# Seven-product layers of a two-block transformer: down products dealt between units, the sixth product added in the second bank, later raw loads and low parts

## The reference, cut to what matters

```
# first block (D_FF = 4096)
x = x + jnp.square(jax.nn.relu(h2 @ w_ff1)) @ w_ff2
# second block, twice (D_FF_2 = 2816)
x = x + (silu(h @ w_gate) * (h @ w_up)) @ w_down
```

## Time and profile before

| | |
|---|---|
| median of 3 runs | 2162.22 us (2161.79 to 2162.78) |
| the profiled execution's own time | 2162.55 us |
| its span, first to last instruction | 2160.8 us |
| TensorE matmuls busy | 2106.1 us, 97% |
| weight loads busy | 1730.6 us, 80% |
| VectorE, ScalarE, GpSimd busy | 1506.4, 1040.7, 416.9 us |
| stage 0, 1, 2 begin near | 569, 1171 and 1790 us of the span |

### The profile page before, as it was taken

The page is one execution under the profiler, slowest core; times in us unless marked ns, Lnnn a source line. Parts: engine busy times, 40 slices in busy tenths (PEclk is TensorE's granted clock), DMA queues, the critical chain, the costliest instruction groups (busy, mean ns, idle before and its releaser), DMA issues.

```text
span 2160.8 us, 31657 instructions
## 1 busy us (share of the span) xinstructions
PE 2106.1 (97%) x12528; PEld 1730.6 (80%) x12528; DVE 1506.4 (70%) x2197; ACT 1040.7 (48%) x1754; POOL 416.9 (19%) x350
## 2 busy tenths in 40 slices
PE   9999999999989999999999999999999999999999
PEld 7768777778769899877777788989877667789988
DVE  5674775655577777665576888887556777888885
ACT  4464445554444343434455445545445564545453
POOL 0000422211112323010010134343011101143340
PEclk9999999999999999999999999999999999999999
DMA  4212112123322232222112323222221113222222
GB/s 171 86 49 88 60 53 93 49 85 114 105 98 96 100 118 89 65 92 69 60 58 77 109 88 118 79 98 79 91 85 60 58 49 107 98 98 90 106 107 69
DMA packets 45938, 187.18 MB, mean 87 GB/s; under 512 B 5216, under 2 KB 5728, under 8 KB 40032
## 3 DMA queue, kind: packets, MB, share of 16 engines
q1 hardware_dynamic: 45648, 184.98, 24.8%
q10 hardware_dynamic: 144, 0.18, 0.0%
HBM read 183.05 MB, written 2.10 MB: 86 GB/s over the span
## 4 chain that ended last, share of the span: by engine, by line
PE 85%; DVE 8%; ACT 3%; issue 2%; DMA 1%; SPq 0%; POOL 0%; DVEq 0%; ACTq 0%
PE ps L1252 14%; PE ps L1255 14%; PE ps L1258 14%; PE ps L1326 7%; PE ps L1332 6%; PE ps L1329 6%; PE ps L1276 4%; PE ps L1279 4%; PE ps L1277 4%; PE ps L1231 3%; PE ps L1384 1%; DMA raw<-in_weights 1%; DVE wl L2129 1%; PE ps L1436 1%; PE ps L1657 1%
## 5 line engine op out<-in xcount | busy, mean ns | idle before, releaser
L1716 ACT CAST wh<-raw 128x1024 fp32r<-128x1024 f32 (+1 forms) x246 | 257.6, 1047 | 419.9 <-PE ps L1258 312.2
L2756 POOL TENSOR_TENSOR Q<-Q 128x512 f32<-128x512 f32 x176 | 280.1, 1592 | 807.4 <-DMA Q<-in_sevens 797.1
L2129 DVE TENSOR_TENSOR wl<-raw,wh 128x1024 fp32r<-128x1024 f32 (+2 forms) x250 | 316.9, 1268 | 161.9 <-ACT wh L1716 161.5
L1252 PE MATMUL ps<-R,wh 128*128 128x512 f32 x892 | 288.2, 404 | 7.3 <-ACT wh L1716 5.4
L1255 PE MATMUL ps<-R,wl 128*128 128x512 f32 x892 | 278.2, 392 | 2.8 <-DVE wl L2129 2.6
L1258 PE MATMUL ps<-R,wh 128*128 128x512 f32 x892 | 276.4, 390 | 0.0
L1252 PE MATMUL ps<-hh,wh 128*128 128x512 f32 x704 | 231.3, 409 | 2.7 <-issue 0.8
L1255 PE MATMUL ps<-hh,wl 128*128 128x512 f32 x704 | 219.4, 393 | 12.5 <-DVE wl L2129 12.5
L1258 PE MATMUL ps<-hl,wh 128*128 128x512 f32 x704 | 217.6, 390 | 0.0
L1255 PEld LDWEIGHTS ps<-R,wl 128*128 128x128 f32 x892 | 167.5, 188 | 41.4 <-DVE wl L2129 5.4
L1252 PEld LDWEIGHTS ps<-R,wh 128*128 128x128 f32 x892 | 159.5, 189 | 48.8 <-issue 10.8
(11 more groups left out here) (281 smaller groups left out, 3697.7 us busy)
## 6 DMA issues: line engine op xcount, KB each, us to landing
raw<-in_weights SPq DMA_DIRECT2D x244, 512.0 KB, 3.5
Q<-in_sevens SPq DMA_DIRECT2D x44, 1024.0 KB, 4.9
x<-in_x_t SPq DMA_DIRECT2D x4, 512.0 KB, 7.0
F<-in_x_t SPq DMA_DIRECT2D x4, 512.0 KB, 4.8
out<-x SPq DMA_DIRECT2D x7, 256.0 KB, 2.0
raw<-in_weights SPq DMA_DIRECT2D x4, 416.0 KB, 3.1
x<-in_bias SPq DMA_DIRECT2D x1, 1024.0 KB, 6.9
F<-in_weights SPq DMA_DIRECT2D x2, 384.0 KB, 3.6
```

What stands on the lines that cost most here:

```text
L1252: pe.matmul(out, hi[:, k, cs], B.tile(u.src, k)[0], start=k == 0, stop=False)
L1716: act.copy(B.wh[s][:, 0:nk * ncol], B.raw[s][:, 0:nk * ncol]).then_inc(S["w_hi"], 1)
L2129: dve.tensor_tensor(lo, src, hi.bitcast(F32), ALU.subtract).then_inc(S[name], 1)
L2756: pool.tensor_tensor(B.weight_part(u.v, out), B.weight_part(u.v, a), B.weight_part(u.v, b), op).then_inc(S["w_s"], 1)
```

## The change: what it does

1. `chain`: the down units of the chunk before are dealt out evenly behind the `Seven` units of the next: stages 1 and 2 run G d U d G d U d. Stage 0 has two up units per chunk and keeps its order.
2. Product 5 is accumulated in q's second half, onto product 3 (no start flag), after the copy out of q. Product 4 is copied out of p by ScalarE (a third `wcp`, 128x256), and product 6 waits for that copy. Three `wc` additions are left of four. Bank 3 is free, and down tiles rotate over four banks instead of three.
3. `tile_low` of ordinary tiles is a step of its own, one piece later, behind that piece's `split_low`.
4. `preparation`: new piece numbers; `wq` and `ws` of the second unit five pieces later in stage 0 and two in stages 1 and 2.

```
@@ gated
+        if u.ev in ("relu2", "fup"):
+            self.defer(1, "tile_low", u)
@@ Plan.seven
-        if k in (2, 5):
-            first.append(("wc", u, {2: 1, 5: 2}[k]))
+        if k == 2:
+            first.append(("wc", u, 1))
         if k == 5:
-            self.defer(1, "wc", u, 3)
+            first.append(("wcp", u, 3))
+            self.defer(1, "wc", u, 2)
...
         if k == 6:
-            self.defer(1, "wc", u, 4)
+            self.defer(1, "wc", u, 3)
@@ preparation
+        plain = stage == 0
+        end = 32 if plain else 48
         for m in range(8):
-            put((13, 14, 15, 17, 18, 19, 21, 22)[m], "hn", v, stage, m)
+            put(((13, 14, 16, 17, 18, 20, 21, 22) if plain else (14, 15, 17, 18, 20, 21, 23, 24))[m], "hn", v, stage, m)
         put(14, "ws", wins[0])
         for k in range(4):
-            put((21, 24, 26, 28)[k], "t_sum", stage, k)
-            put((25, 26, 28, 30)[k], "t_hi", stage, k)
-        end = 32 if stage == 0 else 48
-        for k in range(4):
-            put((29, 33, 34, 35)[k] if stage == 0 else (30, 33, 37, 41)[k], "t_lo", stage, k)
+            put(((22, 24, 25, 27) if plain else (26, 28, 30, 32))[k], "t_sum", stage, k)
+            put(((24, 25, 27, 28) if plain else (28, 29, 31, 33))[k], "t_hi", stage, k)
+            put(((28, 29, 30, 33) if plain else (34, 36, 38, 40))[k], "t_lo", stage, k)
...
             put(end + i, "b_hi", stage, i, last_up)
-            put(end + 1 + i + (3 if stage == 0 else 0), "b_lo", stage, i)
-        put(end + 4, "wq", wins[1])
-        put(end + 4, "ws", wins[1])
+            put(end + 2 + i, "b_lo", stage, i)
+        put(end + (9 if plain else 6), "wq", wins[1])
+        put(end + (9 if plain else 6), "ws", wins[1])
@@ chain
-                n = len(ff[c][0]) // 2
-                out += ff[c][0][:n] + ff[c - 1][1][:2] + ff[c][0][n:] + ff[c - 1][1][2:]
+                n = len(ff[c - 1][1]) // len(ff[c][0])
+                for i, u in enumerate(ff[c][0]):
+                    out += [u] + ff[c - 1][1][n * i:n * i + n]
@@ banks of the down units
-                        u.banks.append(turn % 3)
+                        u.banks.append(turn % 4)
@@ tensor_program.seven
         elif k == 5:
-            empty(3)
+            at.wait_ge("w_cp", 3 * u.v + 2)
         elif k == 6:
-            at.wait_ge("w_c", 4 * u.v + 2)
+            at.wait_ge("w_cp", 3 * u.v + 3)
         out = {0: B.bank[q][:, first], 2: B.bank[q][:, first], 3: B.bank[q][:, second],
-               5: B.bank[3][:, second if half else first]}.get(k, B.bank[p][:, first])
+               5: B.bank[q][:, second]}.get(k, B.bank[p][:, first])
...
-            pe.matmul(out, hi[:, n, :], high[:, n, :], start=n == 0 and k not in (4, 6), stop=False, skip_group_check=True)
+            pe.matmul(out, hi[:, n, :], high[:, n, :], start=n == 0 and k not in (4, 5, 6), stop=False, skip_group_check=True)
@@ seven_copy
-        else:
+        elif n == 2:
             at.wait_ge("w_mm", u.product(3) + 1)
             act.copy(b[:], q).then_inc(S["w_cp"], 1)
+        else:
+            at.wait_ge("w_mm", u.product(4) + 1)
+            act.copy(a[:, 256:512], p[:, 0:256]).then_inc(S["w_cp"], 1)
@@ combine
         elif n == 2:
-            at.wait_ge("w_cp", 2 * v + 2)
-            at.wait_ge("w_mm", u.product(4) + 1)
-            dve.tensor_tensor(a[:, 256:512], p[:, 0:256], b[:, 256:512], ALU.add).then_inc(S["w_c"], 1)
-        elif n == 3:
+            at.wait_ge("w_cp", 3 * v + 3)
             at.wait_ge("w_mm", u.product(5) + 1)
-            at.wait_ge("w_c", 4 * v + 2)
-            dve.tensor_tensor(a[:, 256:512], r, a[:, 256:512], ALU.add).then_inc(S["w_c"], 1)
+            dve.tensor_tensor(a[:, 256:512], q[:, 256:512], a[:, 256:512], ALU.add).then_inc(S["w_c"], 1)
```

More of the change, by code:

```diff
@@ L1303, in seven @@
     def seven(u, k):
-        i, (p, q), half = u.product(k), u.banks(), u.v % 2
+        i, (p, q) = u.product(k), u.banks()
         if k == 0:
@@ L1310, in seven @@
         elif k == 2:
-            at.wait_ge("w_cp", 2 * u.v + 1)
+            at.wait_ge("w_cp", 3 * u.v + 1)
         elif k == 4:
-            at.wait_ge("w_c", 4 * u.v + 1)
+            at.wait_ge("w_c", 3 * u.v + 1)
         elif k == 5:
-            empty(3)
+            at.wait_ge("w_cp", 3 * u.v + 2)
         elif k == 6:
-            at.wait_ge("w_c", 4 * u.v + 2)
+            at.wait_ge("w_cp", 3 * u.v + 3)
         first, second = slice(0, 256), slice(256, 512)
         out = {0: B.bank[q][:, first], 2: B.bank[q][:, first], 3: B.bank[q][:, second],
-               5: B.bank[3][:, second if half else first]}.get(k, B.bank[p][:, first])
+               5: B.bank[q][:, second]}.get(k, B.bank[p][:, first])
         (hi, lo), (high, low), name = B.operand(u.place(i)), B.tokens(PRODUCTS[k][1]), PRODUCTS[k][1]
@@ L1333, in seven @@
         last.then_inc(S["w_mm"], 1)
[L1334 to L1337, removed]
+        if k == 6:
+            emptied[p], emptied[q] = (("w_c", 3 * u.v + 3),), (("w_c", 3 * u.v + 2),)
     def mm(u, i, a, b):
@@ L1859, in seven_sigmoid @@
             at.wait_ge("f_lo", u.others[1].arg["tile"])
-        at.wait_ge("w_c", 4 * u.v + 3 + t)
+        at.wait_ge("w_c", 3 * u.v + 2 + t)
         act.activation(to[:], B.W[u.tiles()[t]][:], ACT.Exp, scale=-1.0).then_inc(S["w_sig"], 1)
@@ L1867, in seven_copy @@
     def seven_copy(u, n):
-        q = B.bank[u.banks()[1]]
+        p, q = (B.bank[b] for b in u.banks())
         a, b = (B.W[i] for i in u.tiles(2 if u.ev == "up" else 0))
@@ L2300, in ev @@
                                          op1=ALU.mult).then_inc(S["ev_d"], 1)
-                tile_low(u, B.W[4 + n % 4])
             elif u.ev == "fgate":
@@ L2309, in ev @@
                 dve.tensor_tensor(w[:], bank[:], w[:], ALU.mult).then_inc(S["ev_d"], 1)
-                tile_low(u, w)
             elif u.ev == "up":
@@ L2323, in ev_low, with tile_low @@
         normed_low(u.arg["norm"], u.arg["m"] + j)
-    def tile_low(u, w):
+    def tile_low(u):
+        w = B.W[4 + u.arg["tile"] % 4 if u.ev == "relu2" else u.arg["wk"]]
         hi, lo = B.pair(("f", u.arg["f"]))
@@ L2365, in combine @@
     def combine(u, n):
-        p = B.bank[u.banks()[0]]
-        r, v = B.bank[3][:, 256:512] if u.v % 2 else B.bank[3][:, 0:256], u.v
+        (p, q), v = (B.bank[b] for b in u.banks()), u.v
         a, b = (B.W[i] for i in u.tiles(2 if u.ev == "up" else 0))
         if n == 1:
-            at.wait_ge("w_cp", 2 * v + 1)
+            at.wait_ge("w_cp", 3 * v + 1)
             at.wait_ge("w_mm", u.product(1) + 1)
@@ L2373, in combine @@
         elif n == 2:
-            at.wait_ge("w_cp", 2 * v + 2)
-            at.wait_ge("w_mm", u.product(4) + 1)
-            dve.tensor_tensor(a[:, 256:512], p[:, 0:256], b[:, 256:512], ALU.add).then_inc(S["w_c"], 1)
-        elif n == 3:
+            at.wait_ge("w_cp", 3 * v + 3)
             at.wait_ge("w_mm", u.product(5) + 1)
-            at.wait_ge("w_c", 4 * v + 2)
-            dve.tensor_tensor(a[:, 256:512], r, a[:, 256:512], ALU.add).then_inc(S["w_c"], 1)
+            dve.tensor_tensor(a[:, 256:512], q[:, 256:512], a[:, 256:512], ALU.add).then_inc(S["w_c"], 1)
         else:
+            at.wait_ge("w_cp", 3 * v + 2)
             at.wait_ge("w_mm", u.product(6) + 1)
@@ L2699, in vector_program @@
             "h_score": h_score, "h_fin": h_fin, "h_low": h_low, "c_norm": c_norm, "c_turn": c_turn, "c_qt": c_qt, "c_kv": c_kv,
-            "c_kt": c_kt, "sb": sb, "dn_sum": dn_sum, "dn_mul": dn_mul, "wo_lo": weight_low, "hn": normed, "t_sum": token_sums, "t_lo": token_low,
+            "c_kt": c_kt, "sb": sb, "dn_sum": dn_sum, "dn_mul": dn_mul, "wo_lo": weight_low, "hn": normed, "t_sum": token_sums, "tile_low": tile_low, "t_lo": token_low,
             "b_lo": part_low, "wc": combine, "wf": seven_value, "wf_lo": seven_low}
```

## The result

The changed kernel takes 2146.28 us, median of 4 runs (2145.89 to 2148.74), beside 2162.36 us for the kernel before on the same chip: a ratio of 0.9927, 95% interval 0.9912 to 0.9942. It is faster by 16.1 us, where I had forecast 29 with a range of 17 to 44. The profiled execution took 2146.68 us with a span of 2145.0, so 15.9 us less than that of before.

What follows compares the result with a forecast made beforehand. TensorE's matmuls, busy 97% of the span, were taken as the bound. Gains of 9.8 + 14.5 + 1.8 + 2.8 = 28.9 us from the profiled 2162.55, less 0.33, gave 2133 us; forecast range 2126 to 2138, chance 0.50.

Steps and rivals of the forecast that it cites:

- stage 0's opening: Stage 0, pieces 9 to 48: later `wq` and earlier chunk low parts win 14.5 us in all.
- stages 1 and 2, pieces 16 to 48: Openings of stages 1 and 2: late low parts of chunks go, winning 5.1 and 6.1 us.
- product 6's waits: Product 6 of U in stages 1 and 2 stops waiting for VectorE, 14 times; all 19.6 us go.
- piece 48 to product 2: From piece 48 to product 2 of the first G, stages 1 and 2: 0.6 us lost in each.
- low clock behind the new waits: After 4.5 us waits at the first G in stages 1 and 2, the clock drops: 2.7 us lost each.
- Dealing the down units: Product 2 of a G behind a down unit waits for a ScalarE copy: 0.7 us at 14 places, 9.8 us lost.
- the prediction's own formula: Lateness of product 2 of G: `split`'s start after VectorE's last addition, plus 1.89, minus 6.76 us.
- Sums in the tail everywhere: Rival: GpSimd's sums stretch U's tail at all 14 places, 1.4 instead of 0.7 us each; 2143 us, chance 0.13.
- Product 5's copy: Product 5 waits for the copy out of q, covered by product 4: nothing; without cover 0.4 us, 44 times.
- The rival that VectorE stays the bound there: Openings: VectorE's work, not its wait, makes low parts late; half of 17.9 us stays; 2142 us, chance 0.10.
- `wq` in stages 1 and 2: Step moves past no `raw` load, so TensorE stands 4.5 us at product 2 of the first G.
- Everything clean: Rival: clock stays up at the 4.5 us waits and the place before G costs nothing; 2119 us, chance 0.20.

Runs made afterwards that it cites:

- the old order: Changed kernel with the down units back in the order G U d d in stages 1 and 2, all else as changed: 2134.58 us, ratio 0.9871.
- `tile_low` alone: Kernel before with only `tile_low` one piece later, preparation's piece numbers unchanged: 2148.26 us, ratio 0.9935.
- before, sixth product: Kernel before with only part 2 of the change (q's second half, third copy, three additions, four banks for down tiles): 2155.48 us, ratio 0.9967.
- before, dealt: Kernel before with only the new `chain`, the dealt order G d U d: 2165.05 us, ratio 1.0013.
- before, `wq` of stage 0: Kernel before with only the second unit's load and sums five pieces later in stage 0: 2154.92 us, ratio 0.9964.
- after, old numbers: Changed kernel with the old piece numbers of `preparation`, `wq` and `ws` staying where the change puts them: 2145.39 us, ratio 0.9920.

## Why the prediction was wrong

The sum, term by term, gains positive, in us of the profiled executions:

| term | predicted | measured |
|---|---|---|
| stage 0's opening | 14.5 | 12.7 |
| stages 1 and 2, pieces 16 to 48 | 5.1 + 6.1 = 11.2 | 4.5 + 5.1 = 9.6 |
| product 6's waits | 19.6 | 20.2 |
| piece 48 to product 2 | -1.2 | -2.4 |
| low clock behind the new waits | -5.4 | -3.7 |
| product 2 behind a down unit | -9.8 | -21.9 |
| elsewhere | 0 | 1.4 |
| sum | 28.9 | 15.9 |

Product 6's 20.2 is what the units lost before; the 21.9 is the 25.6 they lose now less the 3.7 of the clock.

**The step that failed** is "Dealing the down units", where I took 0.7 us for each of 14 places between bounds of 0.5 and 1.4. It cost 21.9 us, so 1.56 a place, and 12.1 of the 13.0 us by which the sum is wrong. By starts the 21.9 split so: 15.5 at the 13 waits of product 2, 1.2 each, and 1.4 more just behind them; 4.3 at 5 places where product 3 stands for a late low part; and the remaining 0.7 in slivers, most of them over the down pieces. So the price of a place was too low (16.9 instead of 9.8 us), and the late low parts of product 3 were a term that I had at nothing.

My way to choose between the bounds was the start of GpSimd's sums: 0.9 us before the last addition in one case, 1.2 after it in the other. I argued that they would now begin in between, and they did, 0.2 us after it in the rows above and 0.2 to 0.6 after it at 10 of the 14 places. What did not follow was a price in between. The sums last 6.4 us and the tail is 6 us long, so a start near the tail's start leaves nearly all of its two-input operations beside them. Only the first of them is a little less stretched (1.44 instead of 1.77). `split` starts 1307.93 - 1301.92 = 6.01 us after the last addition, and 6.0 to 6.4 us after it at those 10 places, beside 6.3 in stage 0 of before. That makes 6.01 + 1.89 - 6.76 = 1.14 us by the prediction's own formula, and product 2 comes 1.11 us late by starts. The formula holds to within 0.03 us at all 14 places, also where the sums begin 2.2 us after the addition, `split` comes after 4.93 us and product 2 is late by 0.04. What was wrong is the 5.6 us or so that I put into it, and not the formula.

The rival "Sums in the tail everywhere", to which I gave 0.13, named this mechanism, and its 2143 is nearer to the result than my 2133. It should have been the forecast: the trace had eight of ten places of stage 0 on its side. The Trainium skill, page SBUF — State Buffer, section Who interferes with whom, says that the instruction which issues first holds the shared ports for its whole length and that the other is fully blocked meanwhile. The 1.44, 1.78 and 2.31 us agree with it: they are 0.75 to 1.09 over what these operations take alone, less than the 6.40 / 4 = 1.6 us of one sum. So do the additions that read PSUM, at 0.69 us beside running sums.

**Product 5's copy** I cost at nothing, with product 4 as its cover. For the changed kernel that came true, but not for the reason given: in the old order the copy stands behind the sigmoid and costs 0.36 us of idle time at 16 places, 10.6 us by starts. The dealt order puts a down unit between G and U, and the sigmoid runs beside it. So this is what dealing does buy, and I named neither the wait nor this gain. The prediction placed the sigmoid "At G" after product 6 and looked for its harm at product 6; it is at product 5 of the U behind that G.

**The openings** were right in mechanism and 3.4 us too good: I left 1 us in stage 0 and 0.5 in stage 2, and two late low parts of 1.54 and 0.89 us are left in stage 0 and about 0.6, 1.5 us in the others (44.09 and 45.03 for 43.52). The rival that VectorE stays the bound there is out: `tile_low` alone takes the late low parts from 15.1 us to 4.8.

**`wq` in stages 1 and 2** went as predicted: moved past no load, so one wait of 4.71 and one of 4.44 us where I had 4.5, both with the clock at 0.50 to 0.55 behind them. The clock cost 2.1 and 1.6 instead of 2.7 each. The way from piece 48 to product 2 grew by 0.93 and 1.45 instead of 0.6. The rival "Everything clean" needed the clock to stay up, and it did not.

**Elsewhere** 1.2 of the 1.4 us lie between the last product 6 of stage 0 and piece 9 of stage 1, 291.55 us instead of 292.71. It is there in every kernel with four banks for down tiles (sixth product alone too, 291.61) and in none of the others on the kernel before (dealt 292.71, `tile_low` 292.72, `wq` of stage 0 292.59). That the fourth bank is the cause, and not the rest of that part, was not tried.

## What to carry to other kernels

A busy interval of one engine that excludes another is not priced by where it starts but by how much of the other's chain it can cover; if it is as long as that chain and starts near its start, take the whole stretch. Ask then what else is queued in order behind the stretched step: moving one cast back in ScalarE's queue was worth 11.5 us with the stretch left in place, while moving the stretch itself lost 6.8. And two edits that remove the same wait are not to be added; look for what each brings in its place, one at a time, on distances between starts rather than on idle time.

## What the runs showed of the hardware that I had not expected

The idle time of a pipelined TensorE leaves out some 0.3 us of what each wait costs, which is about half of a short one. 16 waits with 5.8 us of idle time cost 10.6 us by starts, and 10.1 us of measured time when taken away; 13 waits with 13.45 us of idle time cost 16.9 by starts; and 16 with 23.3 cost 27.8. That is 0.30, 0.27 and 0.28 us a wait more than the idle time.

A single wait of 4.4 us in a stretch in which TensorE is otherwise full was enough for the granted clock to fall to half, as the 5.39 us had done before. Taking the two waits away was worth 11.0 us, 9.4 of it before product 2.

Shorter waits are no safe side. In the kernel before, waits up to 2.2 us left the clock up, and I took that for what such waits do. In other kernels of this study it fell to 0.50 behind waits of 1.5 to 2.9 us: behind 1.51 and 1.84 us in "before, dealt", 1.76 us in "before, `wq` of stage 0", 2.04 and 2.82 us in "after, old numbers", and 1.84, 2.23 and 2.91 us in "before, sixth product". The wait of 2.2 us before the same group of matmuls in stage 0 is there in the kernel before and in three others, and only "before, sixth product" lost the clock behind it. The window behind that wait, columns as in the earlier trace rows, in the kernel before and in "before, sixth product":

```profile
594.00:598.00 4.00, 3.95 (x17) 3.30 (x18) 2.65 (x5) 1.25 (x2) 0.00 (x0) 1.00 0.40 131
594.00:598.00 4.00, 3.91 (x10) 3.09 (x11) 2.65 (x6) 1.25 (x2) 0.00 (x0) 0.57 0.46 133
```

10 matmuls fall into it instead of 17. What decides between the two is not shown by any run here. Such a fall costs little where later waits take it up, but in the profiled execution of "before, dealt" piece 9 of stage 0 starts 1.7 us later than before, behind the one after the wait of 1.51 us.
